# Last stage of a decoder layer on one core: the last column group and the samples accumulate onto copies held in PSUM; last weight units are loaded one by one

## What is computed

```python
def moe_ffn(x, router_w, router_b, w_gate, w_up, w_down):
    ...                       # combine: weight of each expert for each token, two experts a token
    y = jnp.zeros((B * T, D), f32)
    for e in range(N_EXPERTS):
        h = jax.nn.silu(xt @ w_gate[e]) * (xt @ w_up[e])
        y = y + combine[:, e:e + 1] * (h @ w_down[e]).astype(f32)
    return y.reshape(B, T, D).astype(x.dtype)

x = layer_norm(ALPHA * x + moe_ffn(x, ...), ln2_g, ln2_b)
```

## Time and profile before

| | |
|---|---|
| time, median of 3 runs (lowest to highest) | 1657.43 us (1656.62 to 1657.88) |
| time of the profiled execution | 1656.72 us |
| its span in the profile | 1654.9 us |
| PE busy | 1592.7 us, 96% |
| DVE, ACT, POOL busy | 684.9, 391.0, 46.8 us |
| chain that ended last | PE 78%, DMA 19%, DVE 1%, ACT 1% |
| DMA | 543.88 MB, mean 329 GB/s, about 430 GB/s in slices 20 to 38 of 40 |

### The profile page before, as it was taken

The page is one execution under the profiler, slowest core; times in us unless marked ns, Lnnn a source line. Parts: engine busy times, 40 slices in busy tenths (PEclk is TensorE's granted clock), DMA queues, the critical chain, the costliest instruction groups (busy, mean ns, idle before and its releaser), DMA issues.

```text
span 1654.9 us, 25151 instructions
## 1 busy us (share of the span) xinstructions
PE 1592.7 (96%) x11180; PEld 1060.0 (64%) x11180; DVE 684.9 (41%) x1030; ACT 391.0 (24%) x419; POOL 46.8 (3%) x85
## 2 busy tenths in 40 slices
PE   9999999999999999999999998998998899999998
PEld 9999999999999999973532523424334234225334
DVE  7437678657575665544520110111021011102726
ACT  7444555533453333320000000000000000000002
POOL 2000000022000000000000000000000000000000
PEclk9999999999999999999999999999999999999999
DMA  9676576589656769879999999999999999999995
GB/s 265 185 224 171 156 202 171 162 248 324 175 159 185 236 177 344 253 312 417 424 430 432 430 432 431 432 434 432 432 432 432 431 432 431 432 431 431 431 415 174
DMA packets 240709, 543.88 MB, mean 329 GB/s; under 512 B 5072, under 2 KB 218144, under 8 KB 227312
## 3 DMA queue, kind: packets, MB, share of 16 engines
q1 hardware_dynamic: 233536, 524.93, 83.4%
q0 software_dynamic: 4896, 15.49, 2.9%
q10 hardware_dynamic: 2192, 2.20, 0.4%
HBM read 535.65 MB, written 6.95 MB: 328 GB/s over the span
## 4 chain that ended last, share of the span: by engine, by line
PE 78%; DMA 19%; DVE 1%; ACT 1%; issue 0%; SPq 0%; DVEq 0%; ACTq 0%
PE bank L981 16%; PE bank L662 13%; PE bank L663 12%; PE bank L664 12%; PE bank L1075 10%; DMA ring_low<-wu 10%; DMA ring_high<-wu 8%; PE bank L944 5%; PE bank L1153 3%; DMA ring_low<-w_in 2%; PE bank L1109 1%; PE bank L1061 1%; PE bank L716 0%; PE bank L1147 0%; PE bank L998 0%
## 5 line engine op out<-in xcount | busy, mean ns | idle before, releaser
L664 PE MATMUL bank<-x_hi,w_lo 128*128 128x264 f32 x1216 | 344.8, 284 | 0.0
L662 PE MATMUL bank<-x_hi,w_hi 128*128 128x264 f32 x1200 | 344.2, 287 | 0.0
L663 PE MATMUL bank<-x_lo,w_hi 128*128 128x264 f32 x1200 | 340.5, 284 | 0.0
L981 PE MATMUL bank<-ring_low,reg_pk 128*64 128x512 f32 x1248 | 282.2, 606 | 25.3 <-DMA ring_low<-wu 25.3
L1456 DVE TENSOR_TENSOR w_lo<-ring_low,w_hi 128x2048 fp32r<-128x2048 f32 x107 | 244.8, 2289 | 137.2 <-ACT w_hi L1260 136.7
L1260 ACT CAST w_hi<-ring_low 128x2048 fp32r<-128x2048 f32 x107 | 203.8, 1904 | 141.6 <-PE bank L664 86.1
L664 PEld LDWEIGHTS bank<-x_hi,w_lo 128*128 128x128 f32 x1216 | 228.2, 188 | 0.0
L662 PEld LDWEIGHTS bank<-x_hi,w_hi 128*128 128x128 f32 x1200 | 226.6, 189 | 1.8 <-issue 1.3
L663 PEld LDWEIGHTS bank<-x_lo,w_hi 128*128 128x128 f32 x1200 | 226.4, 189 | 0.1
L981 PEld LDWEIGHTS bank<-ring_low,reg_pk 128*64 128x64 f32 x1248 | 88.6, 139 | 212.0 <-issue 171.7
L981 PE MATMUL bank<-ring_high,reg_pk 128*64 128x512 f32 x768 | 175.9, 613 | 22.8 <-DMA ring_high<-wu 20.8
(11 more groups left out here) (385 smaller groups left out, 1697.3 us busy)
## 6 DMA issues: line engine op xcount, KB each, us to landing
ring_high<-wd SPq DMA_DIRECT2D x21, 4096.0 KB, 30.0
ring_low<-wg SPq DMA_DIRECT2D x21, 4096.0 KB, 30.0
ring_low<-w_in SPq DMA_DIRECT2D x76, 1024.0 KB, 5.8
ring_high<-wu SPq DMA_DIRECT2D x14, 4096.0 KB, 23.0
ring_low<-wu SPq DMA_DIRECT2D x14, 4096.0 KB, 25.5
ring_low<-wd SPq DMA_DIRECT2D x7, 4096.0 KB, 31.6
ring_high<-wg SPq DMA_DIRECT2D x7, 4096.0 KB, 30.9
ring_low<-wo SPq DMA_DIRECT2D x16, 1024.0 KB, 7.2
```

The source lines that it names most:

```text
L662: pe.matmul(out, hi[k], of_hi[:, k, :], start=(k == 0), stop=False)
L663: pe.matmul(out, hi[k], of_lo[:, k, :], start=False, stop=False)
L664: mm = pe.matmul(out, lo[k], of_hi[:, k, :], start=False, stop=(k == kk - 1))
L981: mm = pe.matmul(psum[2 * a + part][64 * half:64 * half + 64, :], xg[:, k, CAP * a:CAP * a + CAP], wt[:, kk, 512 * half:512 * half + 512], ...
```

## The change

- **Transfers.** In every pair but the first, units 18 and 19 are two DMAs (`ALONE`); in the last pair units 14 to 19 are six (`LAST_SINGLE`). PE waits for each by itself.
- **Gain rows.** `gain_out` is cut in two: blocks 0 and 1 after unit 18 (PE) with their two copies on ACT there; blocks 2 and 3 in `down_last`.
- **Copies in PSUM.** Before the down blocks PE copies `acc_s` into banks 0 and 1 (two matmuls of 256 columns) and columns 1536 to 2047 of `acc` into banks 2 and 3 (two of 512), by identity matmuls. The last block's scatter and the samples' scatter accumulate on them; `add_part` of block 3 and the sample adds fall away; statistics and gain products read PSUM.
- **Whole-column copies.** ACT copies all 128 rows of each block to `ob`; DVE's `out_part` is gone.
- **Statistics of the samples.** Four matmuls with `twins` (built by POOL) put all four groups' statistics in bank 5, and one aggregation joins them; the two averages and their small operations are gone.
- **Last norm.** Order and banks of `carried` and `shifted` change; the last block of both tiles and block 2 of tile 1 go through `carried` on PE and `scaled` on ACT, which has five now, and DVE three. Fillers go from five to eight and from two to one.
- **Stores.** Tile 1 is stored in two DMAs of 512 KB; the last block of tile 0 is stored by ACT ahead of its two sample stores.

```diff
+LAST_SINGLE = 14
+ALONE = (18, 19)
...
-                for m in range(SINGLES if first else 0, UNITS - 4 if last else UNITS, 2):
+                for m in range(SINGLES if first else 0, LAST_SINGLE if last else UNITS, 2):
                     s = slot_of(m)
+                    if m in ALONE:
+                        for one in ALONE:
+                            sp.wait_ge(w_used, i * UNITS + (W_FREE + one - 7))
+                            sp.dma_start(ring_slot(slot_of(one)), weights(experts, one)).then_inc(landed[slot_of(one)], 16)
+                        continue
...
+                for m in range(LAST_SINGLE, UNITS - 4) if last else ():
+                    sp.wait_ge(w_used, i * UNITS + (W_FREE + m - 7))
+                    sp.dma_start(ring_slot(slot_of(m)), weights(experts, m)).then_inc(landed[slot_of(m)], 16)
...
             store(0, 0, 1)
-            store(1, 1, 1)
-            store(1, 2, 2)
+            store(1, 0, 2, 2)
             store(0, 1, 2)
-            store(1, 0, 3)
+            store(1, 2, 4, 2)
             store(0, 2, 3)
-            store(0, 3, 4)
-            store(1, 3, 4)
...
                         if last and a:
                             scatter_first(i, 4 * part + q - 1)
+                            if 4 * part + q == UNITS - 18:
+                                pe.wait_ge(rows_in, 16 * 8)
+                                gain_out((0, 1)).then_inc(gain_mm, 1)
...
-                gain_out().then_inc(gain_mm, 1)
+                gain_out((2, 3)).then_inc(gain_mm, 1)
+                pe.wait_ge(gain_ev, 2)
+                for half in range(2):
+                    pe.matmul(psum[half][:, 0:256], ident[:, :], acc_s[:, 256 * half:256 * half + 256], start=True, stop=False)
...
                 fill(1, psum[5])
-                hid_transposed(i, 1)
-                fill(2, psum[5])
+                hid_transposed(i, 1, 4)
+                for half in range(2):
+                    at_col = 1536 + 256 * half
+                    pe.matmul(psum[2 + half][:, :].rearrange("p (a n) -> p a n", n=256), ident[:, :], acc[:, :, at_col:at_col + 256], start=True, stop=False)
...
-                carried(0, made + 2)
-                pe.wait_ge(sc_ev, (NPAIR - 1) * N_SC + 8)
-                carried(1, made + 4)
-                carried(2, made + 5)
-                fill(5)
+                pe.wait_ge(sc_ev, (NPAIR - 1) * N_SC + 6)
+                pe.wait_ge(xg_ready, made + 2)
+                carried(1, 0, 6)
+                pe.wait_ge(xg_ready, made + 4)
+                carried(1, 1, 7)
+                fill(8, psum[5])
                 pe.wait_ge(shift_ready, 1)
...
-                fill(2)
+                fill(1, psum[5])
+                sample_stats()
                 pe.wait_ge(shift_ev, 1)
-                shifted(0, 0)
-                shifted(1, 1)
-                shifted(1, 2)
-                pe.wait_ge(sc_ev, NPAIR * N_SC)
-                shifted(0, 3)
-                shifted(1, 0)
-                shifted(0, 1)
-                shifted(0, 2)
-                pe.wait_ge(quarter_ready, 1)
-                pe.wait_ge(y_ready, 1)
-                sample_average(0)
-                carried(3, made + 7)
-                sample_average(1)
-                shifted(1, 3)
+                shifted(0, 0, 4)
+                shifted(1, 0, 6)
+                pe.wait_ge(l_var, 4)
+                shifted(0, 1, 5)
+                shifted(1, 1, 7)
+                pe.wait_ge(xg_ready, made + 7)
+                carried(1, 2, 3)
+                shifted(1, 2, 3)
+                shifted(0, 2, 2)
+                pe.wait_ge(ya_ready, 1)
+                carried(1, 3, 6)
+                shifted(1, 3, 6)
+                pe.wait_ge(ya_ready, 2)
+                carried(0, 3, 7)
+                shifted(0, 3, 7)
...
-                            act.copy(ob[0:64, 256 * c:256 * c + 256], psum[4 + c % 2][0:64, 0:256]).then_inc(lob_act if c < 3 else ob_act, 1)
+                            act.copy(ob[:, 256 * c:256 * c + 256], psum[4 + c % 2][:, 0:256]).then_inc(lob_act if c < 3 else ob_act, 1)
...
+            scaled(1, 0, 6, 2)
+            scaled(1, 1, 7, 4)
             act.wait_ge(l_var, 4)
             act.activation(mv[:, 2, 2:3], mv[:, 2, 1:2], ACT.Sqrt, bias=eps).then_inc(l_std, 1)
-            scaled(3, 8)
+            scaled(1, 2, 3, 5)
+            scaled(1, 3, 6, 7)
+            scaled(0, 3, 7, 8)
+            act.wait_ge(ya_ready, 5)
+            act.dma_start(y[0:P, 1536:2048], acc[:, 0, 1536:2048]).then_inc(y_out, 16)
...
-                    dve.memset(stat[:, 0, 4, 1:2], 1.0)
-                    out_part(i, 0)
-                    for c in range(4):
+                    dve.memset(nm[:, 1:2], 1.0)
+                    for c in range(3):
                         add_part(i, c)
...
+                    for half in range(2):
+                        dve.wait_ge(sc_mm, i * N_SC + (7 + half))
+                        for tt in range(2):
+                            ins = dve.bn_stats(stat[:, tt, 3 + half, :], last_bank(half)[:, tt, :])
...
-                sample_add()
+                for half in range(2):
+                    ins = dve.bn_stats(stat[:, 2, half, :], sample_half(half, own))
+                ins.then_inc(s_part, 1)
+                for half in range(2):
+                    gain_last(half, own)
+                dve.wait_ge(s_avg, 1)
+                dve.bn_aggr(ms[:, 0:2], psum[5][:, 0:48]).then_inc(l_var, 1)
                 scaled(0, 1)
-                scaled(1, 6)
+                scaled(1, 3)
+                gain_part(0, 2)
...
+                scaled(2, 6)
```

More of the change, by code:

```diff
@@ L952, in gather, with unit @@
                     gather_part(p, r)
-            def unit(i, m, first=False, own=False):
+            def unit(i, m, first=False, own=False, last=False):
                 if first and m in once:
@@ L962, in unit @@
                 s = slot_of(m)
-                made = (1 if s >= 4 and not own else 0) + m // 8 + 1
+                if m in ALONE and not first:
+                    pe.wait_ge(landed[s], i * 16 + 48)
+                    return ring_slot(s)
+                if last and m >= LAST_SINGLE:
+                    pe.wait_ge(landed[s], 48)
+                    return ring_slot(s)
+                made = (1 if s >= 4 else 0) + m // 8 + 1
+                if own:
+                    made -= (1, 0, 1, 2)[s // 2]
+                doubles = 2 if s // 2 == 1 else 3
                 if first:
@@ L1117, in down_last @@
                         rows = slice(64 * half, 64 * half + 64)
-                        mm = pe.matmul(psum[4 + half][32 * nn:32 * nn + 32, 0:256], chosen[rows, 2 * P:2 * P + 32], ob[rows, 256 * nn:256 * nn + 256], start=True, stop=True)
+                        mm = pe.matmul(psum[half][32 * nn:32 * nn + 32, 0:256], chosen[rows, 2 * P:2 * P + 32], ob[rows, 256 * nn:256 * nn + 256], start=False, stop=True)
                 mm.then_inc(sc_mm, 1)
@@ L1135, in scatter_last @@
                         rows = slice(64 * half, 64 * half + 64)
-                        mm = pe.matmul(psum[6 + half][:, 256 * tt:256 * tt + 256], chosen[rows, P * tt:P * tt + P], ob[rows, 256 * c:256 * c + 256], start=True, stop=True)
+                        mm = pe.matmul(psum[(6 if c < 3 else 2) + half][:, 256 * tt:256 * tt + 256], chosen[rows, P * tt:P * tt + P], ob[rows, 256 * c:256 * c + 256], start=(c < 3), stop=(c < 3 or tt == 1))
                         if tt:
@@ L1195, in shifted, with sample_stats, carried @@
-            def shifted(tt, c):
+            def sample_stats():
+                pe.wait_ge(twin_ready, 1)
+                pe.wait_ge(s_part, 1)
+                for nn in range(4):
+                    mm = pe.matmul(psum[5][:, 12 * nn:12 * nn + 12], twins[:, nn, :, :].rearrange("p r x -> p (r x)"),
+                                   stat[:, 2, 0:2, :].rearrange("p n s -> p (n s)"), start=True, stop=True)
+                mm.then_inc(s_avg, 1)
+            def carried(tt, c, bank):
+                pe.matmul(psum[bank][:, :], ident[:, :], scaled_acc[:, tt, 512 * c:512 * c + 512], start=True, stop=False)
@@ L1197, in shifted @@
+            def shifted(tt, c, bank):
                 rows = slice(32 * c, 32 * c + 2)
-                pe.matmul(norm_bank(tt, c)[:, :], shift_rows[rows, P * tt:P * tt + P], ln2_rows[rows, :], start=(tt == 0), stop=True).then_inc(rank_two, 1)
+                pe.matmul(psum[bank][:, :], shift_rows[rows, P * tt:P * tt + P], ln2_rows[rows, :], start=(tt == 0 and c < 3), stop=True).then_inc(rank_two, 1)
             def last_norm(made):
-                carried(0, made + 2)
-                pe.wait_ge(sc_ev, (NPAIR - 1) * N_SC + 8)
@@ L1385, in pair @@
                     act.wait_ge(hid_tr, i * 2 + (a + 1))
-                    act.copy(hidt.rearrange("p j f s -> p (j f s)"), psum[2 * a][:, :]).then_inc(hid_ev, 1)
+                    act.copy(hidt.rearrange("p j f s -> p (j f s)"), psum[4 if last and a else 2 * a][:, :]).then_inc(hid_ev, 1)
```

(14 more changed lines are left out.)

142 lines of the change are left out of this document (52 added, 90 removed).

## The result

The changed kernel takes 1665.68 us (median of 5 runs, 1664.61 to 1666.62), the kernel before 1657.43 us (median of 5 runs too, 1656.62 to 1657.88). The ratio is 1.0050, 95% interval 1.0039 to 1.0062: slower, by 8.25 us of medians. The forecast was +4.1 us, 1661.5, with a range up to 1665.5. The direction was right; the size was half of what came, and the result lies 0.2 us beyond the range.

The account below looks back on a forecast made before the run. DMA bounds the loop to 1489.9, then PE's queue. Front +2.1, block 3 and statistics -2.0, fillers +0.75, way to `shifted` +0.65, tail +4.75, end -2.1: +4.15 us, 1661.5 for the median; range 1658.2 to 1665.5.

Parts of the forecast that it names:

- What bounds the kernel: Whole kernel: DMA bounds the loop before 1489.9; behind it each microsecond on PE's queue counts until another engine is later.
- One sign of being wrong: Conditions stated to refute the forecast: PE idling for DVE/ACT in the tail, last chain through SP/DVE, landings moving over 0.5 us.
- Part 1: Up-unit transfers: single DMAs remove PE's idle time in pair 6 but slow the stream; -0.6 us (between -0.7 and +0.7).
- only the idle 0.93 us: Pair 6, before units 18 and 19: single transfers hide just PE's idle 0.93 us, not a unit's work (3.5 us).
- The price of smaller transfers: Transfer stream, five pairs before the hand-over: single units run slower, costing 0.25 to 1.6 us, taken as 0.3.
- Part 2: PE before the down blocks: cut gain matmuls add 1.05 us, copies and the rest 1.65; down block 3 ends 2.1 later.
- if they slip beside the 64-row scatter: Gain matmuls cut in two: lower bound of 0 added cost if they overlap the scatter; upper bound 1.07, taken 1.05 us.
- Part 3: Last block and statistics: shift ready 2.0 us sooner, but fillers hold PE 0.85 us; +0.85 us at the shift's matmuls.
- Part 4: Tail, from the shift's first matmul: longer way to `shifted` +0.65 us, serial order +4.75 us to the last bank.
- About 9.5 us in all: Tail, first `shifted` to last bank: `carried` and `shifted` largely serial on PE, 9.5 us against 4.75 before.
- The rival: Tail: granted clock falls to half near 1648.5, adding +2.7 to +5.3 us, 1664 to 1667; chance 0.2.
- The rule weighed there, on program order: Tail: the skill's strict program order of matmuls would make it 0.45 us longer, 1661.9; the forecast assumed row-group overlap.

Follow-up runs that it names:

- experiment 3: Kernel before plus only the single transfers (units 18 and 19 of each pair but the first, 14 to 19 of the last): 1654.92 us, ratio 0.9987.
- experiment 4: Changed kernel with the transfers of before, the rest kept: 1667.14 us, ratio to before 1.0060.
- experiment 6: Changed kernel with four fillers instead of eight: 1664.73 us, ratio to before 1.0052.
- experiment 1: Changed kernel with each `shifted` matmul feeding 98 rows instead of two, so the output differs: 1660.45 us, ratio to before 1.0021.
- experiment 5: Kernel before plus only the whole-column copies, ACT copying all 128 rows of each down block: 1655.90 us, ratio 0.9994.

## Why the prediction was half right

**What bounds the kernel, and the order of the argument: right.** The last transfer in the chain hands over near 1479, and from there PE's own queue decides. PE doesn't wait for DVE in the tail, and the last chain is PE, ACT, ACT's stores, as forecast. One sign of being wrong did show, landings that move by more than 0.5 us: the last one in the chain came 1.1 us earlier, for a reason told under part 1.

**Part 1: right mechanism, small terms mis-sized.** The step was "only the idle 0.93 us". The idle time of one execution was taken for the price, when it was 9.71 minus a stretch that the clock had lengthened. Experiments 3 and 4 show 1.15 us at the end of unit 19 with the dip and 2.85 without, of which 1.0 to 1.1 last behind the next landing that PE meets. The price of smaller transfers was about right: in the trace of the changed kernel units 18 and 19 land 4.90 and 4.89 us apart, 9.79 together where one double takes 9.71, 0.08 us a pair, 0.4 us over five pairs against the 0.3 taken; by the landings of units 16 and 17 from pair 1 to pair 6 it was 0.6 us in all (583.4 us against 582.8). So the traces give the part -0.5 to -0.7 us, where the forecast had -0.6, and the ratios -2.2 and -1.7.

Of the -2.3 us in the table above 1.2 is the gain at unit 19; the other 1.1 is that units 16 and 17 landed at 1478.99 instead of 1480.11. That lead was there before any single transfer: units 16 and 17 of pair 1 landed at 895.6 in the changed kernel and, one interval of 9.71 us ahead of units 18 and 19 at 907.04, at 897.3 in the kernel before, where one landing near 839 had come 1.7 us late. Still, PE started unit 16 of pair 6 at 1480.15 to 1480.45 in the three profiled executions with doubles and at 1478.56 to 1480.84 in the seven with singles, six of them before 1479.7. Whether this is chance, and whether it is what the ratios show beyond the traces, stays open.

**Part 2: right.** From the last up unit's end to the first down block 4.49 us were measured and 4.5 forecast; the gain pair, cut in two, costs 1.06 each time. The bound of zero "if they slip beside the 64-row scatter" did not occur.

**Part 3: right.** Scatter 3 starts 0.45 us after block 3 ends (0.4 forecast), the four statistics take 1.43 us (1.45 forecast), the fillers hold PE past DVE. The rows, answering to the earlier trace rows:

```profile
1637.54 1.43 DVE L2005 BATCH_NORM_STATS2 small<-bank 128x6 f32<-128x256 f32 x4 [0.29 <-PE bank L1152]
...
1640.49 0.17 DVE L2056 RECIPROCAL small<-small 128x2 f32<-128x2 f32 x1 [0.85 <-ACT small L1443]
```

The fillers were priced at 0.85 us, and experiment 6 gives 0.83.

**Part 4: the step that failed.** "About 9.5 us in all" from the first `shifted` to the last bank. The count is right: of the 15.6 us, 3.16 ran at full clock and 12.45 at half; at full they would be 3.16 + 6.2 = 9.4 us. So the order was read well, and the whole gap of 6.1 us is the clock: the term that failed is the clock, put at full to the end. The prediction had this case as a rival, with 0.2, and let it decide on "PE is never idle in the new tail". That sentence was true (12.43 of 12.45 us) and the conclusion false. Experiment 1 shows it: rows, not idle time, made the difference. The rival was also priced short, +2.7 to +5.3 us, because it let the clock fall no earlier than it had in the kernel before, at 1648.5; it fell 3.2 us after the first `shifted`. With the -2.3 us in the front it came out at 1665.7, inside the 1664 to 1667 of the rival.

What spoke for it was in the earlier trace rows all along: the clock of before fell near 1648.5, just behind small matmuls, with no idle time of PE over a microsecond in the 11 us ahead of it (the last longer one, 1.3 us, had ended at 1636.7). The Trainium skill (TensorE: Matmul & The Clock Gate, section "HAM oscillation — how this bites in real kernels") ties the fall to idle gaps. By that section the clock would have stayed full in this tail, and the time would have been some 6 us less; the stretch 1646.65 to 1659.10 speaks against it, 0.50 with no gap, and the measurement decides.

**The rule weighed there, on program order, was a small matter:** two pairs of `shifted` in two row groups took 2.45 us, the forecast had 2.35 with overlap and 2.8 without, and strictly one after the other they took 3.53 us in experiment 1. Matmuls of different row groups did overlap, as the residual matmuls had in the earlier trace rows.

**The end:** from the last bank to the end of the span 3.7 us instead of the 4.35 forecast. ACT's last issues:

```profile
1659.84 0.36 ACTq L1459 DMA_DIRECT2D y<-reg_qg  x1
1660.25 0.89 ACTq L1462 DMA_DIRECT2D y<-xt  x2
```

The last issue starts near 1660.7 and the span ends 2.1 us later, against the 2.6 us taken from SP's issues.

## What to carry to other kernels

Work that an identity matmul takes off DVE is paid on PE, and in a tail where PE is the bound a bank filled by a copy and a two-row matmul costs two whole passes; keep matmuls of few rows side by side in different row groups and put the copies behind them. When an idle time is to be removed, read it together with the stretch before it, at the clock granted there, and with the next landing that PE will meet: what was a wait of 0.93 us in one execution was 2.62 in others, and 1.55 us of what was freed became a wait for the next transfer. One profile's clock is one sample. And price the clock for every stretch in which PE is fed by few rows, even if it never idles.

## What the runs showed of the hardware that was not expected

- The granted clock fell to half with PE busy without a gap for 10 us before (1636.38 to 1646.65) and stayed there for 12.4 us of gapless matmuls of two rows and copies in turn. The same sequence with 98 rows kept it full.
- A `shifted` of two rows, alone in the array, costs about what one of 98 rows does: two of them 3.71 us at half clock, which would be 1.86 at full, against 1.72 us measured with 98 rows. It is cheap only beside others.
- The half-clock dip of 3.41 us near 1480 follows an idle time of 2.62 us that all ten kernels had there, yet three of their profiled executions (experiments 3, 4 and 5) did not have it. What sets this was not tried.
- ACT copies 128 rows by 256 columns of a bank in 0.37 us, 64 rows in 0.36, and DVE took 0.43 for its 64: a copy split by rows over two engines saves nothing.
